# One fetch of six contiguous rows for both token tiles: re-pitching the relative-position bias table of a neighbourhood-attention layer

## The chip, the cores and the metric

The kernel runs on one core of one Trainium2 chip. The metric is the device time of one execution in microseconds (us). Beside it stands one execution under the hardware profiler. The engines are TensorE (PE, its weight load PEld), VectorE (DVE), ScalarE (ACT), GpSimd (POOL) and SyncE (SP). SP, POOL and ACT also start DMA transfers, which sixteen DMA engines carry out; q1 is the queue of the transfers that SP starts, q0 that of the transfers that POOL starts.

## The reference, cut to what matters

The model is two layers over 256 latent tokens (a grid of 4 rows by 64 columns) of width 1024, with 256 context tokens. The first layer mixes tokens by neighbourhood attention (8 heads of 64) and a short gated convolution; the second by a convolution of 31 taps; each is followed by a mixture of 16 experts. The bias table is used in the attention alone:

```
rpb_c = rpb.astype(jnp.float32)[:, :, dc]          # rpb: (8 heads, 15, 31)
...
    dr = rs + jnp.arange(kr) - r + (NA_KR_MAX - 1)
    bias = jnp.transpose(rpb_c[:, dr], (0, 2, 1, 3))
    s_loc = jnp.einsum("bwhd,brwkhd->bhwrk", q_r, k_nb).astype(jnp.float32) * scale + bias[None]
```

With 4 grid rows every query sees all 4, and the difference of grid rows lies between -3 and 3: seven of the fifteen table rows of a head are used. Inside a grid row a query sees 16 of the 64 columns; the kernel computes all 64 and adds a mask of -1e30 outside.

## The kernel before

Stage one of the kernel is the input projection. Its weights (w_in) and the modulation matrices (w_mod) come in units of 512 KB through one ring of eight slots, in an order written out by hand (FIRST): after the first six weight units, roughly three modulation units go to two weight units. SP issues the loads in that order; each waits until the unit eight places ahead of it has been consumed. ACT rounds a weight unit into whi (line 802), DVE computes the rest wlo (line 1101), and PE multiplies with both. There is room for six rounded units. The modulation vectors 2 to 4 are summed on DVE (lines 1116, 1119), 24 units in all; the others go through PE (line 1626). All three engines work through orders fixed in the program. The blocks of PE in order: two blocks for K (lines 1731 to 1733, the first in a form of its own, lines 1775 to 1777), two for V (lines 1750 to 1752, four tiles of 24 matmuls each), two for Q, two each for the three parts of the convolution (lines 1731 to 1733 again). ACT rounds up to the tenth weight unit (here n9, counted from n0) before it copies the four tiles of the first V block out of PSUM (line 893), rounds n10 and n11 after them, and rounds n12 and n13 only after the last tile of the second V block. PE may not start the second V block before those copies, since it has four PSUM banks for these tiles.

The bias goes this way. POOL loads the seven rows of each head into rpbt (56 partitions, line 722), waits until the second modulation unit is through, and writes rpbt into memory as bias_scratch, every partition 64 times (line 725). When that has landed it fetches bias (line 734): partition q of a half of the tile starts at another offset in bias_scratch, and so gets the table shifted by its column. One fetch covers one head, one token tile and one half, 64 partitions of four rows of 256 B. There are 32 fetches. DVE adds the mask to each head (mask_bias, line 1129), at places in its order given by MASK_AT: heads 0, 1, 2 ahead of n8's rest, 3 and 4 ahead of n9's, 5 ahead of n10's, 6 ahead of n12's, 7 ahead of n14's. The attention adds the bias to the scores (line 1251) and takes their maximum (line 1252). bias lies where the modulation vectors 2 to 5 are placed later; POOL fills vectors 2 to 4 (line 711) when all 16 scores have been multiplied. In the code n16 and so on follow the same count.

After the attention come the output projection, the router and the experts, whose weights stream through the same ring enlarged to 20 slots.

## Time and profile before

| | |
|---|---|
| median of 3 executions | 895.24 us (889.35 to 898.9) |
| the profiled execution | 895.48 us, its span 893.6 us |
| busy in the span: PE, DVE, ACT, POOL | 831.7, 402.4, 241.2, 83.1 us |
| mean granted TensorE clock | 0.96 |
| read from HBM | 291.77 MB |

Times in the rows below are counted from the start of the span. "Busy" counts what an engine executes; a wait shows as the idle time in brackets ahead of an instruction, with what ended it. Landing is the time from the issue of a DMA to the arrival of its data.

### The profile page before, as it was taken

How to read it: one execution, taken by the hardware profiler on the slowest of the kernel's cores; microseconds unless marked ns; L12 is line 12 of the kernel's file. 1: busy time of each engine (PE TensorE's matmuls, PEld its weight loads, DVE VectorE, ACT ScalarE, POOL GpSimd, SP SyncE). 2: the span in 40 equal slices, each digit the busy share in tenths (PEclk: the TensorE clock that was granted, in tenths of full speed). 3: DMA queues.
4: the chain of work that ended last, by engine and by line, in shares of the span. 5: the costliest groups of instructions: out<-in, count | busy, mean ns of one | idle time of the engine just before them, and what ended most of it. 6: DMA issues, size and time to landing. Idle time of an engine off the chain costs nothing.

```text
span 893.6 us, 16817 instructions
## 1 busy us (share of the span) xinstructions
PE 831.7 (93%) x6940; PEld 524.4 (59%) x6940; DVE 402.4 (45%) x682; ACT 241.2 (27%) x449; POOL 83.1 (9%) x154
## 2 busy tenths in 40 slices
PE   5898999999999899999997999989899899999994
PEld 3588995596655355554543987458555445554541
DVE  0476998746522223233336743456702222323334
ACT  3752535623111111111113533443121111111112
POOL 4180000013000000000000344200000000000000
PEclk9999999997799899999997999979899999999997
DMA  9999895869899999999998986599799999999993
GB/s 358 369 260 336 296 366 182 290 200 388 252 393 397 391 398 391 392 354 397 395 398 296 323 244 178 164 369 353 268 386 398 386 398 395 392 376 397 392 397 139
DMA packets 142158, 300.59 MB, mean 336 GB/s; under 512 B 12576, under 2 KB 43584, under 8 KB 142072
## 3 DMA queue, kind: packets, MB, share of 16 engines
q1 hardware_dynamic: 135360, 286.53, 88.5%
q0 software_dynamic: 6384, 12.76, 5.0%
q8 instruction: 59, 0.97, 0.5%
q14 instruction: 27, 0.22, 0.1%
q10 hardware_dynamic: 328, 0.11, 0.0%
HBM read 291.77 MB, written 2.92 MB: 330 GB/s over the span
## 4 chain that ended last, share of the span: by engine, by line
PE 74%; DMA 11%; DVE 8%; ACT 3%; issue 3%; SPq 0%; DVEq 0%; ACTq 0%
PE ps L2024 24%; PE ps L2049 12%; DMA ring<-in_moe_w 6%; PE ps L1975 5%; DMA ring<-in_w_mod 4%; PE ps L1945 3%; PE ps L2114 3%; PE ps L1946 3%; DMA ring<-in_na_w_in 2%; PE ps L1626 2%; PE ps L2140 2%; PE ps L2142 2%; PE ps L2141 2%; DVE wlo L1101 2%; PE ps L1750 1%
## 5 line engine op out<-in xcount | busy, mean ns | idle before, releaser
L2024 PE MATMUL ps<-ring,xg 128*64 128x256 f32 (+1 forms) x2432 | 252.0, 389 | 6.4 <-DMA ring<-in_moe_w 6.1
L2024 PEld LDWEIGHTS ps<-ring,xg 128*64 128x64 f32 (+1 forms) x2432 | 133.8, 129 | 95.3 <-issue 36.9
L1481 DVE SCALAR_TENSOR_TENSOR xres<-ps,gs,xres 128x512 f32<-128x512 f32 x128 | 90.0, 747 | 179.7 <-PE ps L1975 179.7
L2049 PE MATMUL ps<-ring,hidT 128*64 128x512 f32 (+1 forms) x608 | 119.2, 599 | 2.1 <-DMA ring<-in_moe_w 1.7
L2049 PEld LDWEIGHTS ps<-ring,hidT 128*64 128x64 f32 (+1 forms) x608 | 33.5, 128 | 68.9 <-issue 58.3
L1101 DVE TENSOR_TENSOR wlo<-ring,whi 128x1024 fp32r<-128x1024 f32 x56 | 66.6, 1220 | 15.3 <-ACT whi L802 15.2
L802 ACT CAST whi<-ring 128x1024 fp32r<-128x1024 f32 x56 | 56.7, 1046 | 52.4 <-DMA ring<-in_na_w_in 36.3
L969 ACT COPY xg<-ps 128x384 f32<-128x384 f32 (+2 forms) x44 | 20.6, 469 | 145.3 <-PE ps L1946 145.3
L1626 PE MATMUL ps<-ring,pair 128*32 128x256 f32 x576 | 47.2, 448 | 11.4 <-DMA ring<-in_w_mod 7.5
L1465 DVE TENSOR_TENSOR yg<-ps,g2keep 128x512 f32<-128x512 f32 x32 | 21.6, 689 | 74.0 <-PE ps L2049 74.0
L1945 PE MATMUL ps<-pick,hthi 128*128 128x192 f32 (+1 forms) x192 | 52.5, 310 | 0.0
L1945 PEld LDWEIGHTS ps<-pick,hthi 128*128 128x128 f32 x192 | 39.0, 203 | 16.4 <-issue 14.1
L1946 PE MATMUL ps<-pick,htlo 128*128 128x192 f32 (+1 forms) x192 | 48.0, 285 | 0.0
L982 ACT ACTIVATE silu<-ps 128x256 f32<-128x256 f32 x32 | 11.6, 382 | 124.7 <-PE ps L2024 124.7
L1459 DVE TENSOR_TENSOR hid<-silu,ps 128x256 f32<-128x256 f32 x32 | 12.9, 420 | 69.8 <-ACT silu L982 69.7
L1731 PE MATMUL ps<-hThi,whi 128*128 128x256 f32 (+1 forms) x144 | 42.4, 295 | 0.1
L1975 PE MATMUL ps<-yhi,spread 64*128 64x512 f32 (+1 forms) x152 | 37.4, 489 | 5.0 <-DVE ylo L1471 5.0
L1733 PE MATMUL ps<-hTlo,whi 128*128 128x256 f32 (+1 forms) x144 | 42.0, 291 | 0.0
L1732 PE MATMUL ps<-hThi,wlo 128*128 128x256 f32 (+1 forms) x144 | 41.9, 291 | 0.0
L988 ACT COPY hidT<-ps 128x256 f32<-128x256 f32 (+1 forms) x26 | 11.0, 422 | 114.6 <-PE ps L1996 114.6
L1946 PEld LDWEIGHTS ps<-pick,htlo 128*128 128x128 f32 x192 | 39.0, 203 | 1.0 <-issue 1.0
L2140 PE MATMUL ps<-fThi,whi 128*128 128x256 f32 x128 | 36.4, 285 | 0.7 <-DVE fTlo L1536 0.7
(265 smaller groups left out, 1311.9 us busy)
## 6 DMA issues: line engine op xcount, KB each, us to landing
ring<-in_moe_w SPq DMA_DIRECT2D x384, 512.0 KB, 11.6
ring<-in_w_mod SPq DMA_DIRECT2D x96, 512.0 KB, 7.4
ring<-in_na_w_in SPq DMA_DIRECT2D x24, 512.0 KB, 9.5
ring<-in_cf_pw_w SPq DMA_DIRECT2D x24, 512.0 KB, 8.2
ring<-in_ab_w_out SPq DMA_DIRECT2D x8, 512.0 KB, 5.1
mods<-mod_scratch POOLq DMA_DIRECT2D x8, 512.0 KB, 6.9
urep<-uT SPq DMA_DIRECT2D x64, 35.5 KB, 3.4
urep<-uT POOLq DMA_DIRECT2D x64, 35.5 KB, 3.2
```

Of the source, the lines that this page charges most:

```text
L802: A.copy(whi[:, n % SPL, :], raw_unit(u)).then_inc(w_rounded, 1)
L1101: V.tensor_tensor(wlo[:, n % SPL, :], raw_unit(u), whi[:, n % SPL, :], ALU.subtract).then_inc(unit_done, 1)
L1481: V.scalar_tensor_tensor(out=dst, in0=ps[:, plan.spread_banks(m, i)[half], :], scalar=gs[:, t, place:place + 1], in1=dst, op0=ALU.mult, op ...
L1626: ins = T.matmul(ps[q * QUAD:(q + 1) * QUAD, bank, 0:QW], pair[:, k, :], raw_unit(u)[:, q * QW:(q + 1) * QW], start=(k == 0), stop=(k == K ...
L1731: T.matmul(dst, wpart(n0, k, 0, m * P, P), acts(k, 0), start=(k == 0), stop=False)
L1733: i3 = T.matmul(dst, wpart(n0, k, 0, m * P, P), acts(k, 1), start=False, stop=(k == KC - 1))
L1945: T.matmul(dst, hthi[:, t, k * P:(k + 1) * P], sel, start=(t == 0), stop=False)
L1946: ins = T.matmul(dst, htlo[:, t, k * P:(k + 1) * P], sel, start=False, stop=(t == NT - 1))
L1975: ins = T.matmul(ps[:, plan.spread_banks(m, i)[half], :], spread[rows, m % 2, a, t * P:(t + 1) * P], part[rows, a, :], start=(a == 0 and p ...
L2024: ins = T.matmul(ps[lo:lo + width, BW[a], c0:c0 + 2 * P], tile[:, k, o:o + width], raw[:, p.slot(u), w0:w0 + 2 * P], start=(q == 0 and kk ...
L2049: ins = T.matmul(ps[lo:lo + width, BY[a], :], hidT[:, a, o:o + width], raw[:, p.slot(u), half * HALF:(half + 1) * HALF], start=(q == 0), s ...
L2140: T.matmul(dst, wpart2(done_n, k, 0, m * P, P), a0, start=(k == 0), stop=False)
```

## The change

The seven used rows of a head now lie one behind the other on one partition of rpbt (8 partitions of 512 elements), each 64 elements from the next (GRID_W, where the old layout gave a row 128 and a partition of its own). bias_scratch becomes 8 x 64 x 512. Since the rows of a head are at a pitch of 64, four grid rows by 64 columns are 256 contiguous elements, and the windows of the two token tiles overlap in one run of six rows, 384 elements: one fetch per head and half serves both tiles. There are 16 fetches of 64 partitions by one run of 1536 B. The tile has 384 elements a head instead of 512 (12 KB instead of 16 KB a partition), and the second tile reads at an offset 128 elements lower than the first. One DMA instead of eight loads the table. Since the last heads now lie under vector 4, its fill waits until the last bias has been added (biased) as well.

```
-        rpbt = at("rpbt", [HEADS * 7, P], 48)
+        rpbt = at("rpbt", [HEADS, BAND], 48)
...
-        bias = at("bias", [P, HEADS, NT, SEQ], 2 * D * 4 / 1024, base=mods_at)
+        bias = at("bias", [P, HEADS, NEAR * GRID_W], 2 * D * 4 / 1024, base=mods_at)
...
-            for h in range(HEADS):
-                eng.dma_start(rpbt[h * 7:(h + 1) * 7, 48:48 + 2 * KCOL - 1], na_rpb[0, h, 4:11, :]).then_inc(rpb_in, 16)
-            eng.wait_ge(rpb_in, 16 * HEADS)
+            bands = rpbt[:, GRID_W - KCOL:GRID_W - KCOL + OFFS * GRID_W].rearrange("h (r c) -> h r c", r=OFFS)[:, :, 0:2 * KCOL - 1]
+            eng.dma_start(bands, na_rpb[0, :, 4:4 + OFFS, :]).then_inc(rpb_in, 16)
+            eng.wait_ge(rpb_in, 16)
             eng.wait_ge(tensor_unit, 2 * KC)
-            eng.dma_start(bias_scratch, rpbt[:].unsqueeze(1).broadcast_to([HEADS * 7, GRID_W, P])).then_inc(rpb_out, 16)
+            eng.dma_start(bias_scratch, rpbt[:].unsqueeze(1).broadcast_to([HEADS, GRID_W, BAND])).then_inc(rpb_out, 16)
             def load_bias(h):
-                for t in range(NT):
-                    for half in range(2):
-                        src = bass.AP(tensor=bias_scratch.tensor, offset=(h * 7 + 3 - 2 * t - half) * GRID_W * P + GRID_W - 1,
-                                      ap=[[P - 1, GRID_W], [GRID_W * P, ROWS], [1, GRID_W]])
-                        dst = bias[half * GRID_W:(half + 1) * GRID_W, h, t, :].rearrange("p (r c) -> p r c", r=ROWS)
-                        eng.dma_start(dst, src).then_inc(bias_in[h], 16)
+                for half in range(2):
+                    src = bass.AP(tensor=bias_scratch.tensor, offset=h * GRID_W * BAND + (1 - half) * GRID_W + GRID_W - 1,
+                                  ap=[[BAND - 1, GRID_W], [1, NEAR * GRID_W]])
+                    eng.dma_start(bias[half * GRID_W:(half + 1) * GRID_W, h, :], src).then_inc(bias_in[h], 16)
...
             for v in range(2, 5):
+                if v == 4:
+                    eng.wait_ge(biased, 2 * HEADS)
                 mod_fill(v, mods[:, v * D:(v + 1) * D])
...
-                eng.wait_ge(bias_in[h], 64)
-                full = bias[:, h].rearrange("p t (r c) -> p (t r) c", r=ROWS)
-                mask = cst[:, C_MASK:C_MASK + GRID_W].unsqueeze(1).broadcast_to([P, NT * ROWS, GRID_W])
+                eng.wait_ge(bias_in[h], 32)
+                full = bias[:, h].rearrange("p (r c) -> p r c", r=NEAR)
+                mask = cst[:, C_MASK:C_MASK + GRID_W].unsqueeze(1).broadcast_to([P, NEAR, GRID_W])
                 V.tensor_tensor(full, full, mask, ALU.add).then_inc(bias_masked, 1)
...
-                link(V.tensor_tensor(local, local, bias[:, h, t, :], ALU.add))
+                link(V.tensor_tensor(local, local, bias[:, h, 2 * (1 - t) * GRID_W:2 * (1 - t) * GRID_W + SEQ], ALU.add))
```

The new constants are OFFS = 7, NEAR = 6 and BAND = 512; P is 128, ROWS is 4.

## Rows read from the trace of the kernel before

**Rows 1.** The chain that ended last, from 60 to 77 us: start, us, what.
```profile
54.60 20.74 DMA ring<-in_na_w_in
...
76.32 0.37 ACT vv L893
```

**Rows 2.** Timeline of ACT, 60 to 78 us; in brackets idle time and what ended it.
```profile
75.37 1.04 ACT L802 CAST whi<-ring 128x1024 fp32r<-128x1024 f32 x1 [8.60 <-DMA ring<-in_na_w_in]
```

**Rows 3.** Timeline of PE (matmuls), 71 to 90 us.
```profile
72.34 0.28 PE L1751 MATMUL ps<-wlo,hThi 128*128 128x256 f32 x1
72.45 0.28 PE L1752 MATMUL ps<-whi,hTlo 128*128 128x256 f32 x1
76.83 0.36 PE L1750 MATMUL ps<-whi,hThi 128*128 128x256 f32 x1 [4.10 <-ACT vv L893]
```

**Rows 4.** Windows: stretch, length, busy (count) of PE, PEld, DVE, ACT, POOL, clock, DMA share, GB/s.
```profile
48.00:72.50 24.50, 24.41 (x155) 21.66 (x153) 16.62 (x16) 8.04 (x11) 19.83 (x32) 1.00 1.03 260
76.80:119.20 42.40, 42.37 (x354) 41.31 (x355) 36.01 (x41) 17.73 (x30) 0.63 (x1) 0.96 0.95 332
119.20:140.00 20.80, 20.79 (x174) 18.64 (x173) 19.99 (x37) 7.13 (x11) 0.60 (x1) 1.00 0.78 277
```

**Rows 5.** The same view, in stretches of 2 us after PE's stop.
```profile
76.00:78.00 2.00, 1.17 (x9) 1.20 (x10) 1.56 (x2) 1.50 (x5) 0.00 (x0) 0.92 1.06 394
78.00:80.00 2.00, 2.00 (x11) 2.00 (x11) 2.00 (x3) 1.05 (x1) 0.00 (x0) 0.50 1.04 379
80.00:82.00 2.00, 2.00 (x15) 2.00 (x14) 2.00 (x3) 0.00 (x0) 0.00 (x0) 0.73 1.06 378
```

**Rows 6.** DMA view, 49.1 to 75.4 us: totals, queues, bias fetches.
```profile
DMA packets 3693, 6.83 MB, mean 260 GB/s; under 512 B 673, under 2 KB 2488, under 8 KB 3691
...
q1 hardware_dynamic: 2625, 4.63, 68.9%
q0 software_dynamic: 1066, 2.17, 34.4%
...
bias<-bias_scratch POOLq DMA_DIRECT2D x32, 64.0 KB, 7.0
```

**Rows 7.** DMA view, 75.4 to 89 us: totals.
```profile
DMA packets 2949, 5.21 MB, mean 383 GB/s; under 512 B 159, under 2 KB 2186, under 8 KB 2948
```

**Rows 8.** Timeline of POOL around the write and the fetches.
```profile
32.14 1.70 POOL L725 DMA_DIRECT2D bias_scratch<-rpbt  x1 [22.07 <-PE ps L1626]
49.06 19.83 POOL L734 DMA_DIRECT2D bias<-bias_scratch  x32 [13.20 <-DMA bias_scratch<-rpbt]
175.87 1.81 POOL L711 DMA_DIRECT2D mods<-mod_scratch  x3 [30.31 <-PE ps L1616]
```

**Rows 9.** DMA view, 37 to 43 us: POOL's queue (packets, MB, share of 16 engines).
```profile
q0 software_dynamic: 373, 1.25, 58.0%
```

**Rows 10.** Timeline of DVE around 88 us, the instructions before and after its idle time.
```profile
85.64 0.68 DVE L1129 TENSOR_TENSOR bias<-bias,cst 128x512 f32<-128x512 f32 x1
90.97 1.23 DVE L1101 TENSOR_TENSOR wlo<-ring,whi 128x1024 fp32r<-128x1024 f32 x1 [4.65 <-ACT whi L802]
```

**Rows 11.** The instructions that touch bias: durations min/median/max ns, first and last start.
```profile
L1251 DVE TENSOR_TENSOR ps<-ps,bias x16: 421/426/433, 126.6 to 177.8; 128x256 f32<-128x256 f32 x16
L1129 DVE TENSOR_TENSOR bias<-bias,cst x8: 683/685/691, 62.1 to 100.4; 128x512 f32<-128x512 f32 x8
```

**Rows 12.** Timeline of DVE, 178 to 204 us.
```profile
178.28 0.69 DVE L1252 TENSOR_REDUCE smx<-ps 128x1 f32<-128x512 f32 x1
203.34 1.23 DVE L1171 TENSOR_TENSOR htok<-xres,mods 128x1024 f32<-128x1024 f32 x1
```

**Rows 13.** The page's DMA issues: the fills of the modulation vectors.
```profile
mods<-mod_scratch POOLq DMA_DIRECT2D x8, 512.0 KB, 6.9
```

**Rows 14.** Windows, columns as in rows 4: the router's end, and the experts.
```profile
230.00:240.00 10.00, 10.00 (x74) 7.23 (x75) 5.55 (x18) 1.87 (x3) 0.00 (x0) 0.77 0.56 205
300.00:380.00 80.00, 77.25 (x588) 39.81 (x588) 23.66 (x36) 10.44 (x23) 0.00 (x0) 0.96 1.04 394
```

More of the change, by code:

```diff
@@ L22 @@
 ROWS = SEQ // GRID_W
+OFFS = 2 * ROWS - 1
+NEAR = OFFS - 1
+BAND = 8 * GRID_W
 HEADS = 8
@@ L2266 @@
     args.append(nc.dram_tensor("in_consts", [P, C_N], F32, kind="ExternalInput").ap())
-    args.append(nc.dram_tensor("bias_scratch", [HEADS * 7, GRID_W, P], F32, kind="Internal").ap())
+    args.append(nc.dram_tensor("bias_scratch", [HEADS, GRID_W, BAND], F32, kind="Internal").ap())
     args.append(nc.dram_tensor("mod_scratch", [MODS, D], F32, kind="Internal").ap())
```

## The prediction

> **What bounds the kernel now.** I read the chain that ended last first, in the stretch where the bias is made and fetched. From 54.60 to 75.34 us it stands on one DMA, a unit of w_in that took 20.74 us to land; then come ACT's rounding of it and ACT's copy of V out of PSUM [rows 1]. ACT's timeline says the same: it sat idle 8.60 us for that unit (n9) [rows 2]. ACT copies the first V tiles only after n9, and PE needs those copies, so PE stops at the end of the first V block: its last matmul starts at 72.45, the next at 76.83 [rows 3]. The matmuls there start 0.11 us apart [rows 3], so PE could have gone on at 72.57: 4.26 us are lost. Then the clock: in the 6 us after the stop the granted clock was 0.92, 0.50 and 0.73 [rows 5], after full clock up to the stop [rows 4]. At full clock the missing shares, 0.08, 0.50 and 0.27 of 2 us each, are 1.7 us. So the stop costs PE 4.26 + 1.7 = 6.0 us.
>
> Second, the windows on both sides. From 48 to 72.5 PE is busy 24.41 of 24.50 us, and from 76.8 to 119.2 it is busy 42.37 of 42.40 [rows 4]. So nothing else is to be had from PE there, and nothing stands between the stop and 119 us that could swallow what the stop gives back. From 119.2 to 140 DVE is the full one, 19.99 of 20.80 us. DVE's own timeline shows where it last had room: it idles 4.65 us until 90.97, and what ends that is ACT's rounding of n12 [rows 10], which in ACT's order comes behind the last copy of the second V block, that is, behind PE. DVE's order from there on is work without a gap, hung on a point set by PE. If PE is 6 us earlier, so is that point.
>
> Third, why n9 is late. From 49.1 to 75.4 us the DMA engines are full, yet move 260 GB/s [rows 6]; as soon as the bias fetches are in, they move 383 GB/s [rows 7]. In that stretch lie the 32 fetches, 64 KB each in rows of 256 B.
>
> **The fetches, removed and added.** Before: 32 x 65.5 KB = 2.10 MB, in 8192 rows. The stretch of 26.3 us moved 6.83 MB, so 4.73 MB of other data, which at 383 GB/s need 12.3 us. The fetches therefore cost 14.0 us of all DMA engines (at 383 GB/s they would cost 5.5). After: 16 x 98.3 KB = 1.57 MB in 1024 rows of 1536 B. Lower bound, at 383 GB/s: 4.1 us; the rate of rows 7 was reached mostly by rows of w_in, 1 KB each, so rows of 1.5 KB are near that end, and I take 4.5. Upper bound, if the price goes by bytes as it does now: 14.0 x 1.57/2.10 = 10.5 us. So 9.5 us of DMA time come free, at least 3.5, and all ahead of n9's landing. n9 was issued at 54.60, which stays; it lands at about 66 instead of 75.34, at the worst at 71.8. The limit for PE is 72.57 less ACT's chain from landing to PE, 76.83 - 75.34 = 1.49 us, so 71.1. The likeliest value clears it by 5 us, and the upper bound misses it by 0.7 us. The stop goes, and with it most likely the dip in the clock, since the rows show it only behind the stop. On PE: -6.0 us; at the upper bound -3.5 to -5.3.
>
> POOL issues 16 fetches instead of 32, at 0.62 us each [rows 8] about 9.9 instead of 19.83 us, so the last fetch goes out about 10 us earlier; nobody stands behind it in POOL's queue until the first modulation row, tens of us later. Nothing on the path.
>
> **The write to bias_scratch.** Before: issued at 32.14, landed when the first fetch goes at 49.06 [rows 8]. It shrinks from 56 x 64 rows of 512 B (1.84 MB) to 8 x 64 rows of 2 KB (1.05 MB), but it reads 8 partitions instead of 56. In the middle of the write q0 moved 1.25 MB in 6 us, 208 GB/s, with 58% of the engines, so 22 GB/s for each busy engine [rows 9]. No row shows such a write from 8 partitions. The lower bound is by bytes, 16.9 x 0.57 = 9.6 us. If at most eight engines can take part, each has 131 KB, just what 14 engines had each in the write before, and the write takes about as long as now. I take 14 to 17 us, so the fetches begin between 46 and 49: cost nought, at most 1 us of gain, since the bias is not what n9 waits for. The upper bound is by partitions: 208 x 8/56 = 30 GB/s, 35 us. That is a rival below. The Trainium skill speaks against this part of the change ("SBUF — State Buffer", section on the DMA port swizzle): DMA bandwidth goes by the SBUF ports that the partitions reach, 27 GB/s each; 56 partitions reach eight ports, partitions 0 to 7 two. By that estimate the write would need 19 us at 54 GB/s and land near 56. The 208 GB/s of rows 9 lie just under its figure for eight ports, 218, so this trace cannot refute it.
>
> **Loading the table.** One DMA instead of eight on POOL, which waits for PE until 32.14 afterwards anyway, 22.07 us idle [rows 8]. Nothing.
>
> **The masks.** 128x512 took 0.685 us, 128x256 took 0.426 [rows 11]; a straight line gives 0.556 for 384 elements, 0.13 us less for each of eight. Six or seven fall where DVE waits anyway (ahead of 90.97), one, head 7's, in the full stretch: -0.13 us. The addition at line 1251 keeps its shape.
>
> **The new wait.** POOL now holds the fill of vector 4 until the last maximum, which ends at 178.97 [rows 12] where it went out at about 177.1 (third of three from 175.87, rows 8): 2 us later. Behind it on POOL's queue are the move of vector 5, whose row DVE makes only during the output projection, and what follows it. Vector 4 is first read at 203.34 [rows 12]; with a landing of 6.9 us [rows 13] it is there at about 187. Cover 16 us, cost nought; without that cover it would be the 2 us.
>
> **Does the gain reach the end?** From 230 to 240 the DMA engines are only 0.56 busy while the router finishes: the expert units that may be fetched early are in, and the ring stands full. From there the experts run at 394 GB/s with a full DMA [rows 14], a fixed amount of work hung on the router's end. An earlier router moves all of it. So the sum: -6.0 - 0.1 = -6.1 us against the profiled execution's own 895.48, which lies 0.2 above the median. Forecast 895.24 - 6.2 = 889.0 us.
>
> **Rivals.**
> (A) The fetches cost by bytes, so the change does only part of what it says: -3.5 to -5.3, 890 to 892 us. For it: the DMA engines' records give q0 34.4% for its 2.17 MB, no worse per byte than q1 [rows 6]. Against: then the rate would not have leapt from 260 to 383.
> (B) The gain is taken over by DVE and the ring. From 76.8 to 119.2 DVE is busy 36.0 of 42.4 and the DMA share is 0.95 [rows 4]; with 6 us less on the clock, the slots may not be full when n12 is due, and DVE waits for loads instead. The check: DVE reached the point ahead of n12 at 86.32 [rows 10] and n12 would be due at 84.9; it must gain 1.4 us, and it is given 9.5 us of DMA. If only half the gain survives, 892; if none, 895.
> (C) Slower: the write is paced by the partitions it reads. At 30 GB/s it lands near 71 instead of 49. The first three heads come 11 us later, 82 (six fetches issued at 0.62 us, and 7.0 us to land, rows 6 and 8). DVE stands at their masks, in its order ahead of n8's rest; from those masks to n9's rest it has 7.6 us of work (five masks at 0.56, two rests and two modulation units at about 1.2 each), so PE's Q block starts at 89.5, no earlier than now, and DVE, with another 8.2 us until n12 (two rests, four modulation units, two masks), comes there at 98 instead of 90.97: +7, 902 us. It decides from a landing at about 65 on (33 us after issue, against 16.9 now): up to there DVE's idle time pays. The port rule of the Trainium skill lands the write at 56, short of that point, where the bias's lateness costs DVE nothing; the ring's loads on the engines that read those partitions would be held up, and n9 would land at about 71 to 72. By it the time would be 889 to 892; its chance is one in six.
> (D) The stop's removal brings more, because earlier landings also shorten later waits: against it stand the full rows of PE on both sides. 884 to 887.
>
> **Chances.** Forecast as it stands (887 to 891) 0.52; A and the mild form of the write together 0.20; B 0.12; C 0.05; D 0.11. Single executions differ by 1% (889.35 to 898.9), so about 1% is what a measurement can tell from no change, and medians may be off by 2 to 3 us. The range of 8 in 10 is 884 to 895.5: it leaves out C, the worst of B and the far end of D. Faster by over 1% (under 886.3) 0.22, within 1% 0.72, slower by over 1% 0.06.
>
> **What would show it.** In the profile after: 16 fetches; the stretch from 50 to 70 us at 350 GB/s or more; no wait of 8.60 us of ACT at n9; PE busy 2.00 of 2.00 through 72 to 77 with the clock at 1.00 up to 84; the first rounding after the second V block at 83.8 instead of 89.89; the last addition of bias at 171.7 instead of 177.8. A landing of the write after 56, or a wait of DVE at the masks, would show C or its mild form; an idle DVE between 85 and 119 would show B. The prediction is wrong altogether if the stop is gone and the end has not moved.

## The result, and the profile after

The changed kernel took 898.53 us (median of 20 executions, 889.83 to 902.9), the kernel before 893.19 (20 executions on the same chip, 885.17 to 900.0). The ratio is 1.0057, with a 95% interval of 1.0033 to 1.0082: slower by 0.6%, where 0.7% faster was forecast. The profiled execution took 900.92 us, its span 899.2, that is 5.6 us more than before.

POOL's timeline of the changed kernel answers to [rows 8]; in brackets idle time and what ended it.

```profile
32.55 0.82 POOL L728 DMA_DIRECT2D bias_scratch<-rpbt  x1 [25.56 <-PE ps L1629]
58.10 8.68 POOL L735 DMA_DIRECT2D bias<-bias_scratch  x16 [22.66 <-DMA bias_scratch<-rpbt]
184.63 0.53 POOL L714 DMA_DIRECT2D mods<-mod_scratch  x1 [2.27 <-DVE smx L1255]
```

The write is issued at 32.55 and has landed by 58.10, after 25.3 us in the DMA view, where it took 16.6 before, although it carries 1.05 MB instead of 1.84. The fetches are half as many and are out in 8.68 us instead of 19.83, as forecast. The third line is the new wait ahead of vector 4's fill, 2.27 us long.

What the DMA engines did meanwhile stands in the DMA view from 38 to 50 us (queues: packets, MB, share of the time of 16 engines).

```profile
DMA packets 936, 1.89 MB, mean 158 GB/s; under 512 B 208, under 2 KB 588, under 8 KB 935
q0 software_dynamic: 361, 0.83, 51.7%
q1 hardware_dynamic: 574, 1.05, 26.1%
```

The same stretch of the kernel before, for comparison, since no row ahead of the prediction shows it:

```profile
DMA packets 1486, 3.80 MB, mean 317 GB/s; under 512 B 168, under 2 KB 737, under 8 KB 1485
q0 software_dynamic: 641, 2.24, 59.7%
q1 hardware_dynamic: 844, 1.55, 37.1%
```

q0 holds about the same share of the engines (52% against 60%) and moves 0.83 MB with it instead of 2.24. And q1, the ring's queue, falls from 1.55 to 1.05 MB. The write is not only slow, it makes the ring slow. The windows of the changed kernel answer to [rows 4, 5] (stretch, length, busy (count) of PE, PEld, DVE, ACT, POOL, clock, DMA share, GB/s):

```profile
44.00:46.00 2.00, 2.00 (x7) 1.51 (x6) 1.39 (x5) 2.00 (x5) 0.00 (x0) 0.50 0.75 104
50.00:60.00 10.00, 10.00 (x44) 8.09 (x44) 2.02 (x2) 0.84 (x2) 1.90 (x4) 1.00 0.71 160
74.00:76.00 2.00, 0.00 (x0) 0.00 (x0) 0.37 (x1) 1.44 (x3) 0.00 (x0) 0.50 1.06 361
76.00:78.00 2.00, 1.86 (x8) 1.86 (x9) 2.00 (x3) 1.43 (x3) 0.00 (x0) 0.50 1.10 362
78.00:80.00 2.00, 2.00 (x12) 2.00 (x11) 2.00 (x5) 0.19 (x1) 0.00 (x0) 0.50 0.92 343
80.00:82.00 2.00, 2.00 (x16) 2.00 (x16) 1.79 (x2) 0.97 (x2) 0.00 (x0) 0.79 0.93 336
82.00:119.20 37.20, 37.20 (x328) 36.12 (x327) 33.25 (x40) 15.55 (x28) 0.62 (x1) 1.00 0.90 309
```

From 76.14 on PE is full again, as it was from 76.83 on before; full clock comes back at 82. SP's timeline says how the slow write reaches the ring. After:

```profile
35.79 14.33 SPq L607 DMA_DIRECT2D ring<-in_w_mod  x2
50.16 5.43 SPq L611 DMA_DIRECT2D ring<-in_na_w_in  x1
55.63 2.99 SPq L607 DMA_DIRECT2D ring<-in_w_mod  x1
58.66 0.43 SPq L611 DMA_DIRECT2D ring<-in_na_w_in  x1
```

Before:

```profile
49.40 0.38 SPq L608 DMA_DIRECT2D ring<-in_na_w_in  x1
50.53 0.33 SPq L604 DMA_DIRECT2D ring<-in_w_mod  x1
51.67 0.38 SPq L608 DMA_DIRECT2D ring<-in_na_w_in  x1
```

These are the units n7 and n8. SP's issue of n7, 0.38 us long before, takes 5.43 us, and n8 goes out at 58.66 instead of 51.67. The chain that ended last, which answers to [rows 1], now runs through n7:

```profile
48.52 1.64 DVE wlo L1104 x2
50.16 24.37 DMA ring<-in_na_w_in
74.58 0.92 issue
75.51 0.59 ACT kT L890
76.14 0.58 PE ps L1753
```

n7 needs 24.37 us to land; before it needed 8.8. ACT's timeline (answers to [rows 2]), the casts of n6 and n7 and what stands behind them:

```profile
62.35 1.05 ACT L805 CAST whi<-ring 128x1024 fp32r<-128x1024 f32 x1 [0.78 <-DMA ring<-in_na_w_in]
74.56 1.04 ACT L805 CAST whi<-ring 128x1024 fp32r<-128x1024 f32 x1 [11.16 <-DMA ring<-in_na_w_in]
75.51 1.07 ACT L890 COPY kT<-ps 128x512 f32<-128x512 f32 x2
```

ACT rounds n6 and n7 between the second and the third copy of K out of PSUM, so the last two copies wait for n7. PE's timeline (answers to [rows 3]):

```profile
68.93 0.28 PE L1755 MATMUL ps<-whi,hTlo 128*128 128x256 f32 x1
76.14 0.58 PE L1753 MATMUL ps<-whi,hThi 128*128 128x256 f32 x1 [6.94 <-ACT kT L890]
```

So the stop is not gone. It stands after two of the four tiles of the first V block instead of at the block's end, and it has grown: PE could have gone on at 69.04 (0.11 us behind its last matmul) and goes on at 76.14, 7.10 us against 4.26. It goes on a little earlier than before, but with two more tiles ahead of it. The clock is at 0.50 from 74 to 80 and at 0.79 to 82. DVE's timeline (answers to [rows 10]):

```profile
77.97 1.49 DVE L1132 TENSOR_TENSOR bias<-bias,cst 128x384 f32<-128x384 f32 x3
92.57 0.55 DVE L1132 TENSOR_TENSOR bias<-bias,cst 128x384 f32<-128x384 f32 x1
96.33 1.23 DVE L1104 TENSOR_TENSOR wlo<-ring,whi 128x1024 fp32r<-128x1024 f32 x1 [3.21 <-ACT whi L805]
```

The rest of n12 starts at 96.33 instead of 90.97: 5.36 us later. And the instructions that touch bias (answers to [rows 11]; min/median/max ns, first and last start):

```profile
L1132 DVE TENSOR_TENSOR bias<-bias,cst x8: 550/551/554, 78.0 to 105.8; 128x384 f32<-128x384 f32 x8
L1254 DVE TENSOR_TENSOR ps<-ps,bias x16: 421/425/433, 132.0 to 183.2; 128x256 f32<-128x256 f32 x16
```

The first addition of bias starts at 132.0 instead of 126.6, the last at 183.2 instead of 177.8. Both are 5.4 us later, and the span is 5.6 us longer: in this pair of executions the whole loss is made before 97 us.

Not all of it is the stop. PE resumes its first K block at 42.34 instead of 41.95 (0.39 us). The longer stop adds 2.84 us and the longer stretch at a low clock behind it some 0.65 (2.35 us of missing clock against 1.7). The rest, 1.7 us, is a dip of the clock from 42 to 48 us (0.82, 0.50 and 0.82; the first window above shows its middle), which this execution has and the one of the kernel before has not. The four make 5.6 us, against the 5.4 of n12. The dip comes and goes with the execution, as e8 and e12 show below, so these two profiles put some 3.5 us of the loss on the longer stop. The medians of 20 executions are 5.3 us apart, and how often each kernel has the dip isn't known.

### The profile page after: what moved, and what is told of

It is laid out like the page before. It is cut to its first block, busy times and chain, and to the rows that moved or that the text cites. A ratio compares the mean times of both kernels' runs of the same rounds, so it can differ in the third digit from the quotient of the medians.

```text
span 899.2 us, 16795 instructions
## 1 busy us (share of the span) xinstructions
PE 830.7 (92%) x6940; PEld 523.6 (58%) x6940; DVE 401.1 (45%) x682; ACT 241.7 (27%) x449; POOL 67.9 (8%) x131
## 4 chain that ended last, share of the span: by engine, by line
PE 70%; DMA 14%; DVE 9%; issue 3%; ACT 3%; SPq 0%; DVEq 0%; ACTq 0%
PE ps L2027 23%; PE ps L2052 12%; DMA ring<-in_moe_w 6%; PE ps L1978 5%; DMA ring<-in_w_mod 4%; PE ps L2117 3%; PE ps L1948 3%; DMA ring<-in_na_w_in 3%; PE ps L1949 2%; PE ps L1629 2%; PE ps L2143 2%; PE ps L2145 2%; PE ps L2144 2%; PE ps L1753 1%; PE ps L1754 1%
## 5 line engine op out<-in xcount | busy, mean ns | idle before, releaser
L2052 PE MATMUL ps<-ring,hidT 128*64 128x512 f32 (+1 forms) x608 | 121.1, 605 | 1.7 <-DMA ring<-in_moe_w 1.2
L1629 PE MATMUL ps<-ring,pair 128*32 128x256 f32 x576 | 44.6, 429 | 12.9 <-DMA ring<-in_w_mod 8.8
L1948 PE MATMUL ps<-pick,hthi 128*128 128x192 f32 (+1 forms) x192 | 49.0, 295 | 0.0
L1948 PEld LDWEIGHTS ps<-pick,hthi 128*128 128x128 f32 x192 | 36.8, 191 | 16.4 <-issue 14.1
L1949 PE MATMUL ps<-pick,htlo 128*128 128x192 f32 (+1 forms) x192 | 45.0, 274 | 0.0
L1949 PEld LDWEIGHTS ps<-pick,htlo 128*128 128x128 f32 x192 | 36.7, 191 | 0.5 <-issue 0.5
```

The lines of the kernel that those rows point to most:

```text
L1629: ins = T.matmul(ps[q * QUAD:(q + 1) * QUAD, bank, 0:QW], pair[:, k, :], raw_unit(u)[:, q * QW:(q + 1) * QW], start=(k == 0), stop=(k == K ...
L1948: T.matmul(dst, hthi[:, t, k * P:(k + 1) * P], sel, start=(t == 0), stop=False)
L1949: ins = T.matmul(dst, htlo[:, t, k * P:(k + 1) * P], sel, start=False, stop=(t == NT - 1))
L2052: ins = T.matmul(ps[lo:lo + width, BY[a], :], hidT[:, a, o:o + width], raw[:, p.slot(u), half * HALF:(half + 1) * HALF], start=(q == 0), s ...
```

## The experiments

Two questions were open: why the write takes 25.3 us, and what the fetches would bring without it. For the write, theory G says that it is paced by groups of four neighbouring partitions that it reads: partitions 0 to 7 are two groups. Theory N says that the number of partitions counts, or that each of eight engines has its share. Theory F puts the loss on the fetches, whose longer rows would hold the engines longer. The table gives what each run showed. "Landing" is the time from the issue of the write to its landing in the DMA view, "38 to 50" and "50 to 60" are the rates of all transfers in those stretches (in most runs the second is that of the fetches), "n12" the start of its rest on DVE, "first add" that of line 1251's (1254's) first instruction. The ratio is to the kernel before on the same chip.

| kernel | landing us | 38 to 50, GB/s | 50 to 60, GB/s | n12 | first add | ratio [95%] |
|---|---|---|---|---|---|---|
| before | 16.6 | 317 | 268 | 90.97 | 126.6 | 1 |
| after | 25.3 | 158 | 160 | 96.33 | 132.0 | 1.0057 [1.0033, 1.0082] |
| e1, every 4th partition | 12.6 | 318 | 238 | 87.39 | 123.2 | 0.9917 [0.9882, 0.9952] |
| e2, every 2nd | 14.9 | 264 | 260 | 87.09 | 122.9 | 0.9909 [0.9876, 0.9943] |
| e9, every 16th | 15.2 | 279 | 251 | 85.23 | 120.9 | 0.9941 [0.9920, 0.9962] |
| e3, before with 8 partitions | 40.9 | 121 | 61 | | 153.8 | 1.0315 [1.0265, 1.0364] |
| e4, 16 copies | 10.5 | 363 | 266 | 88.58 | 124.2 | 0.9931 [0.9900, 0.9962] |
| e7, e4 with rows 2048 B apart | 9.6 | 355 | 282 | | 122.1 | one execution |
| e5, 16 copies, 128-partition fetch | 13.9 | 384 | 378 | 86.48 | 122.1 | 0.9945 [0.9918, 0.9972] |
| e8, copies, old fetch | 11.4 | 380 | 249 | 87.79 | 123.4 | 0.9999 [0.9966, 1.0033] |
| e12, e8 again | 11.5 | 382 | 257 | 87.40 | 123.0 | 0.9950 [0.9910, 0.9990] |
| e10, 4 copies, 128-partition fetch | 13.7 | 384 | 377 | 86.34 | 122.2 | 0.9908 [0.9869, 0.9947] |
| e11, after with ACT's copies first | 25.6 | 144 | 158 | | 129.3 | 0.9985 [0.9948, 1.0023] |
| e13, before again | 16.7 | 318 | 266 | 91.88 | 127.5 | one execution |

**e1: the same eight partitions' worth of data on partitions 0, 4, ..., 28.** Bytes, rows, fetches and the number of source partitions are those of the changed kernel.

```
-        rpbt = at("rpbt", [HEADS, BAND], 48)
+        rpbt = at("rpbt", [HEADS * 4, BAND], 48)
...
-            bands = rpbt[:, GRID_W - KCOL:...
+            bands = rpbt[0:HEADS * 4:4, GRID_W - KCOL:...
...
-            eng.dma_start(bias_scratch, rpbt[:].unsqueeze(1)...
+            eng.dma_start(bias_scratch, rpbt[0:HEADS * 4:4].unsqueeze(1)...
```

> The changed kernel, with the eight heads' rows of the table on partitions 0, 4, 8 ... 28 instead of 0 to 7; the same 8 partitions of source, the same 1.05 MB, nothing else. Theory G (the write is paced by the groups of neighbouring partitions that it reads; partitions 0 to 7 are two groups of four, here it is eight): the changed kernel's write took 25.3 us from issue to landing, here it takes 10 to 15 us, lands at 43 to 48, and the ring keeps over 300 GB/s between 38 and 50 us instead of 61 to 257. ACT no longer waits 9 us for a weight unit at 50 us. PE's stop shrinks; the time is that of the kernel before or up to 6 us under it, 887 to 893, ratio to before 0.994 to 1.000. Theory N (eight source partitions mean that eight DMA engines carry the whole write, wherever they lie): the landing stays within 2 us of 25.3 and the ratio stays at 1.006. Theory F (the longer runs of the fetch are what hurts): likewise no change.

POOL's timeline of e1, then its window and an issue of SP's:

```profile
32.51 0.82 POOL L728 DMA_DIRECT2D bias_scratch<-rpbt  x1 [25.52 <-PE ps L1629]
45.42 8.47 POOL L735 DMA_DIRECT2D bias<-bias_scratch  x16 [10.03 <-DMA bias_scratch<-rpbt]
```

```profile
38.00:50.00 12.00, 10.11 (x38) 7.68 (x37) 9.32 (x23) 11.97 (x22) 4.58 (x9) 0.86 0.92 318
```

```profile
49.73 0.38 SPq L611 DMA_DIRECT2D ring<-in_na_w_in  x1
```

and the ring's queue from 38 to 50 us in the DMA view:

```profile
q1 hardware_dynamic: 1044, 2.07, 51.5%
```

The spacing alone takes the landing from 25.3 to 12.6 us, the rate from 158 to 318 GB/s and SP's issue of n7 back to 0.38 us; the ring's queue moves 2.07 MB instead of 1.05. PE has no wait of half a microsecond or more from 45 to 125 us. The kernel is 0.8% faster than before, with the fetches as the change makes them, and faster than expected (0.994 to 1.000). This execution has the dip of the clock from 42 to 48 us too, as the changed kernel's had, so the two compare directly: n12 comes 8.94 us earlier by the spacing alone. F falls: the same fetches stand here. N falls too, since there are eight source partitions in both.

**e2: partitions 0, 2, ..., 14.** The edit is e1's with 2 in place of 4; it reads four groups.

> As the kernel with heads at every fourth partition, but on partitions 0, 2, 4 ... 14: four groups of four instead of two (changed kernel) or eight. Theory G: by the two-group write (25.3 us, of which some 5 are fixed and 20 go by the rate) half of 20 and 5 fixed, a landing 14 to 17 us after issue, between the other two or equal to the eight-group one if the engines, not the groups, are the limit by then. Theory N: 25 us.

```profile
47.41 8.80 POOL L735 DMA_DIRECT2D bias<-bias_scratch  x16 [12.29 <-DMA bias_scratch<-rpbt]
```

The write, issued at 32.23, landed after 14.9 us, between the two. The time does not tell it from e1.

**e3: the kernel before, its table on eight partitions.** Fetches, bytes (1.84 MB) and everything else stay those of before; only a head's seven rows lie on one partition, at the old pitch of 128.

```
-        rpbt = at("rpbt", [HEADS * 7, P], 48)
+        rpbt = at("rpbt", [HEADS, 7 * P], 48)
...
-            eng.dma_start(bias_scratch, rpbt[:].unsqueeze(1).broadcast_to([HEADS * 7, GRID_W, P])).then_inc(rpb_out, 16)
+            eng.dma_start(bias_scratch, rpbt[:].unsqueeze(1).broadcast_to([HEADS, GRID_W, 7 * P])).then_inc(rpb_out, 16)
...
+                                      ap=[[7 * P - 1, GRID_W], [P, ROWS], [1, GRID_W]])
```

> The kernel before with one thing of the change alone: the table lies on partitions 0 to 7 (seven rows of 128 elements each) and the write reads these 8 partitions; the bytes written stay at 1.84 MB and the 32 fetches of four rows of 256 B stay as they were. Theory G: 1.84/1.05 x 20 + 5 = 40 us from issue to landing instead of 16.6, the ring crawls for as long, DVE stands at the first masks, time 10 to 20 us above before, ratio 1.01 to 1.025. Theory F: as before, within 0.3%, since the fetch is unchanged. Theory N gives the same as G here if eight engines are slow in themselves.

POOL's timeline of e3 up to 90 us (27 of the 32 fetches), and its window in the middle of the write:

```profile
73.62 17.02 POOL L734 DMA_DIRECT2D bias<-bias_scratch  x27 [38.24 <-DMA bias_scratch<-rpbt]
```

```profile
50.00:60.00 10.00, 10.00 (x46) 8.20 (x45) 2.03 (x2) 1.05 (x1) 0.00 (x0) 1.00 0.49 61
```

The write takes 40.9 us, the kernel 3.15% more, beyond the 1 to 2.5% that were expected. This is the loss by itself, without any other part of the change: PE stops for 14.9, 4.1 and 6.4 us. It also gives the price. After and e3 both read two groups; 0.52 and 0.92 MB a group took 25.3 and 40.9 us, so 0.393 MB more took 15.6 us: 25 GB/s a group, and some 4.5 us besides. For four groups that gives 0.262 / 0.0252 + 4.5 = 14.9 us, as measured in e2, and for eight groups 9.7. e1 measured 12.6; the DMA share is 0.92 there, so the write probably waits for the ring's transfers as well, which no run separates.

The Trainium skill ("SBUF — State Buffer", the section on the DMA port swizzle) gives 27 GB/s for each port and puts partitions 0 to 7 on two of them; the 25 GB/s of these runs agree. It also says that partitions 32 apart share a port.

**e9: partitions 0, 16, ..., 112.** By G in its plain form these are eight groups, as in e1. By the port map just named they are four ports, as in e2.

```
-            bands = rpbt[:, ...
+            bands = rpbt[0:HEADS * 16:16, ...
```

> The changed kernel with the heads at every sixteenth partition, 0, 16 ... 112. If any spacing of four or more gives each head a way of its own, the write lands 12.6 us after issue as with every fourth partition, and from 38 to 50 us 318 GB/s are moved. If the SBUF's groups are those of the Trainium skill (page SBUF - State Buffer, the DMA port swizzle: partitions 32 apart share a port, so these eight reach four ports), it lands as with every second partition: 14.9 us, 264 GB/s. On the time no difference that can be measured, ratio 0.988 to 0.996.

```profile
38.00:50.00 12.00, 10.08 (x44) 7.88 (x43) 9.32 (x22) 11.97 (x21) 2.25 (x5) 1.00 0.89 279
```

15.2 us and 279 GB/s are e2's figures (14.9, 264), not e1's (12.6, 318). So it is the port map's grouping that counts, not nearness as such. These are differences of 2.6 us and 39 GB/s between single executions. DVE's timeline of e9 at the place of [rows 10]:

```profile
85.23 1.23 DVE L1104 TENSOR_TENSOR wlo<-ring,whi 128x1024 fp32r<-128x1024 f32 x1 [3.06 <-ACT whi L805]
```

90.97 to 85.23 is -5.74 us. The first and the last addition of bias come 5.7 us earlier (120.9, 172.1), and the span, 888.0, is 5.6 us shorter.

**e4: sixteen copies of the table on 128 partitions,** each written four times: the same bytes, from every group.

```
+COPIES = 16
...
+            for i in range(COPIES):
+                bands = rpbt[i:P:COPIES, ...
...
+            eng.dma_start(bias_scratch.rearrange("h (i j) b -> (h i) j b", i=COPIES), rpbt[:].unsqueeze(1).broadcast_to([P, GRID_W // COPIES, BAND])).then_inc(rpb_out, 16)
```

> The changed kernel, but the table is loaded 16 times, so that a head's rows stand on 16 neighbouring partitions (128 in all), each written 4 times; the same 1.05 MB in memory, the same fetches. Theory G and N both: all engines and all groups take part, the write lands 7 to 12 us after issue. The difference to the kernel with every fourth partition tells what the engine count adds: under G alone nothing or 1 to 3 us of landing. Time: if the fetches of 1.5 KB cost 5 us less of all DMA engines than before (8.8 against 14.0 of the trace), PE's stop of 4.3 us and the dip of its clock mostly go: 887 to 890, ratio 0.993 to 0.997. If the fetches are no cheaper, ratio 0.999 to 1.001.

The fastest write but one, 10.5 us, and no better time than e1. The sixteen small loads of the table cost time at the start: the second modulation unit is through later, the write went out at 34.40 instead of 32.55, n7 at 51.72 instead of 49.40, and that moves everything behind it. In the five runs with sixteen loads (e4, e5, e7, e8, e12) PE resumes its first K block 1.5 to 2.3 us later than before, in e10 with four loads 0.5; by which way the loads do it, no run shows. The rate while the fetches run stays low:

```profile
50.00:60.00 10.00, 10.00 (x46) 8.19 (x45) 9.00 (x8) 5.51 (x8) 3.58 (x7) 1.00 1.05 266
```

266 GB/s, and 238 in e1, are what the kernel before had (268) with rows of 256 B; the prediction had hoped for 350 or more from rows of 1536 B. Two theories: L, the rows start 2044 B apart in memory and are not aligned; H, each fetch fills 64 partitions, that is half of the groups.

**e7: e4 with the fetched rows 2048 B apart.** This leaves out the shift of the bias from partition to partition, so that every partition gets the same window.

```
-                                  ap=[[BAND - 1, GRID_W], [1, NEAR * GRID_W]])
+                                  ap=[[BAND, GRID_W], [1, NEAR * GRID_W]])
```

> The run with 16 copies, with the fetched rows 2048 B apart instead of 2044, so that all rows of a fetch start at the same place within 256 B. It leaves out the shift of the bias from partition to partition, so its scores are not those of the reference. Theory L: the fetch stretch goes from 266 to 350 GB/s or more. Theory H: it stays at 240 to 280.

```profile
50.00:60.00 10.00, 9.92 (x44) 7.84 (x43) 8.52 (x8) 4.72 (x7) 1.75 (x4) 1.00 1.05 282
```

282 GB/s: alignment brings 16 of the 117 GB/s that are missing to the 383 of [rows 7]. L falls as the main cause. The one execution took 890.07 us.

**e5: e4 with every row written 128 times** (2.10 MB), so that one fetch can fill 128 partitions. There are eight fetches of 192 KB, with the same bytes and rows.

```
+                src = bass.AP(tensor=bias_scratch.tensor, offset=h * P * BAND + P - 1,
+                              ap=[[BAND - 1, P], [1, NEAR * GRID_W]])
+                eng.dma_start(bias[:, h, :], src).then_inc(bias_in[h], 16)
```

> The run with 16 copies, but with 128 instead of 64 repetitions of a head's row in memory (2.1 MB written from 128 partitions), so that one fetch of 128 partitions by 1536 B replaces the two of 64: 8 fetches in all. Theory H (a fetch into 64 partitions reaches half of the groups of partitions and so holds all DMA engines to about 250 GB/s): the stretch of the fetches shows 350 GB/s or more. Theory L (the rows start off a boundary, since they lie 2044 B apart): it stays at 240 to 280 GB/s. On the time nothing, since PE has no stop left between 48 and 125 us in the run with 16 copies: ratio 0.991 to 0.996.

```profile
50.00:60.00 10.00, 9.90 (x44) 7.81 (x43) 8.57 (x9) 5.47 (x8) 1.96 (x4) 1.00 1.05 378
```

378 GB/s, as H expects. The fetches are also half as many and twice as large as in e4, and the memory rows are repeated 128 times; no run keeps their number and widens them alone, so that it is the partitions reached is the likeliest reading and not shown by itself. At that rate the 1.57 MB cost 4.2 us, the 4.5 that the prediction took. The time is 0.55% below before's and no better than e1's: the stop was gone already, and a DMA queue that is faster still releases nobody. n12 stands at 86.48, 4.49 us earlier; PE resumed its first K block, after a wait of 1.9 us inside it that all kernels have, 1.46 us later than before (43.41 against 41.95), again with the sixteen loads, so the stop itself gave back 5.95.

**e8: the write spread, the fetches of before.** Table on 128 partitions in 16 copies, 1.84 MB, 32 fetches of 64 KB.

```
-            eng.dma_start(bias_scratch, rpbt[:].unsqueeze(1).broadcast_to([HEADS * 7, GRID_W, P])).then_inc(rpb_out, 16)
+            eng.dma_start(bias_scratch.rearrange("h (i j) b -> (h i) j b", i=16), rpbt[:].unsqueeze(1).broadcast_to([P, GRID_W // 16, 7 * P])).then_inc(rpb_out, 16)
```

> The kernel before with its 32 fetches of four rows of 256 B, its 16 KB tile and its 1.84 MB of bytes written, but the table stands on 128 partitions (16 copies of each head) for the write, as in the run with 16 copies. It separates the two halves of the change: against that run (ratio 0.993) it differs in the fetch, against the kernel before in the write alone. If the shorter fetches of the change are worth what the trace suggests (DMA cost 14 us before, some 9 after), PE still stops at the V blocks here: write landed 3 us earlier than before at most, ratio to before 0.996 to 1.000, ACT waits 5 us or more at n9. If the gain of the run with 16 copies came from the write alone, the ratio here is 0.993 too and PE doesn't stop.

The write landed after 11.4 us instead of 16.6, and the profile shows no stop of PE: n9 is rounded from 73.6 on instead of 75.37, and PE itself is later, since it resumed the first K block 1.57 us later and then had the dip of the clock (1.7 us from 44 to 48). But the ratio is 0.9999, with executions from 882.61 to 899.52: the ratio is that of the first case of the expectation, the trace that of the second. The profiled one was the fastest of them, so its trace says little of the median.

**e12: e8 once more,** to see where its spread is made: in this stage, by a stop that comes and goes (S), or elsewhere (T).

> The run with the old fetch and the write from 128 partitions once more, since its profiled execution (882.6 us, no stop of PE, n9 rounded at 67.58) was its fastest of 12, and its median was that of before. Theory S: with the old fetch n9 lands within a few us of the limit of 71, so that some executions have the stop and others not; a slower execution under the profiler should then show n9 rounded after 71 and PE idle. Theory T: the spread is made elsewhere; then the profile shows no stop again even at 890 us or more, and the longer time is in the experts' stretches.

The rounding at 67.58 is that of n8; n9's is the one at 73.6.

PE's timeline of e12 shows the one wait from 45 to 125 us:

```profile
74.87 0.36 PE L1751 MATMUL ps<-whi,hThi 128*128 128x256 f32 x1 [0.65 <-ACT vv L894]
```

The windows from 44 to 46 us of e8 and of e12, which are the same kernel:

```profile
44.00:46.00 2.00, 2.00 (x7) 1.57 (x6) 1.78 (x6) 2.00 (x5) 0.64 (x2) 0.54 1.05 278
44.00:46.00 2.00, 2.00 (x10) 1.66 (x9) 1.77 (x7) 2.00 (x6) 0.67 (x2) 1.00 1.05 284
```

One execution has the dip of the clock in the first K block, the other has not.

A median of 890.85 and 0.995. The two profiled executions differ by 8.7 us in span (880.8, 889.5) and by 0.4 us at the first addition of bias; from 640 to 880 us PE is busy 223.9 us in one and 232.5 in the other. So the difference of these two is made in the experts (T). What the write alone is worth in the median stays open between nothing and 0.9%. In this stage it takes nearly all of the stop away by itself, with the old fetches in place: n9, issued 1.58 us later than before, is in 1.97 us earlier, e12 keeps 0.76 of the 4.26 us of idle PE, and no low clock follows.

**e10: both halves put right at a lower price:** four copies of each head on every fourth partition, 128 repetitions, eight fetches of 128 partitions, four table loads.

```
+                bands = rpbt[4 * i:P:4 * COPIES, ...
...
+            eng.dma_start(bias_scratch.rearrange("h (i j) b -> (h i) j b", i=COPIES), rpbt[0:P:4].unsqueeze(1).broadcast_to([HEADS * COPIES, P // COPIES, BAND])).then_inc(rpb_out, 16)
```

> The version that the runs point to. Each head's rows stand on four partitions, every fourth of the 128, so the write reads all sixteen groups with 32 partitions and the table needs four small loads instead of sixteen; 128 repetitions in memory (2.1 MB) and 8 fetches of 128 partitions by 1536 B, as in the run with the full fetch. The write lands 9 to 14 us after issue, the fetch stretch runs at 350 GB/s or more, PE has no stop from 48 to 120 us. Ratio to before 0.989 to 0.995, against the kernel with every fourth partition no difference that can be told; if the sixteen small loads cost the full-fetch run 1 to 2 us at its start, this one gets them back.

0.9908, 886.17 us: the lowest ratio of all, and not to be told from e1's 0.9917, which needs three changed lines. Landing (13.7 us), fetch stretch (377 GB/s) and PE without a stop are as expected.

**e11: the changed kernel with ACT's order turned,** a test of how the slow write reaches PE. All K copies go ahead of the rounding of n6 and n7, and two V copies ahead of n8 and n9.

```
-                if n % 2 == 1:
-                    round_upto(6 + n + 1)
+                if n == 3:
+                    round_upto(8)
...
+                if n == 1:
+                    round_upto(10)
```

> The changed kernel, its slow write and all, with the order of ACT altered: the last K copies out of PSUM come ahead of the rounding of n6 and n7, and the first two V copies ahead of n8 and n9. In the changed kernel PE stood 6.94 us for such a copy, which was queued behind the wait for n7 (landed at 74.5). If that order is what turns a late unit into lost time, PE now runs through the first V block to about 72 and stops only until n7's rest at about 77: 2 to 4 us come back, ratio to before 1.001 to 1.004. If the lateness of the units costs by itself, whatever the order, the ratio stays at 1.006.

The timeline of PE in e11, its longest wait:

```profile
77.89 0.38 PE L1755 MATMUL ps<-whi,hThi 128*128 128x256 f32 x1 [3.28 <-DVE wlo L1106]
```

The write is as slow as ever (25.6 us, 144 GB/s), but the stop falls from 6.94 to 3.28 us, now for n7 itself, with three short ones behind it (0.90, 1.30 and 0.37 us), and the clock stays at 1.00 from 76 to 84 us. The first addition comes at 129.3 instead of 132.0, and the ratio is 0.9985, better than the 1.001 to 1.004 expected. Against the changed kernel's 1.0057, which was measured beside other executions of before, that is 0.7% less. Of the 1.4% that lie between the changed kernel and e1 that is about half (by ratios whose intervals are 0.25 to 0.37% wide to each side), and at the first addition it is 2.7 of 8.8 us. So a part of the loss comes by the copies' place in ACT's order, and the rest by the late landing itself.

**e13: the kernel before, a second look.**

> The kernel before, unchanged, for a second look: whether its stop of PE at 72.5 us (4.26 us, with the dip of the clock behind it) is there in another execution. Theory S allows 2 to 8 us of stop and a time that follows it; theory T expects 4 us again whatever the time.

The stop is there again: PE is idle for 3.90 us until 76.88, and the clock is 0.50 from 76 to 82. 896.48 us, n12 at 91.88 (90.97), the first addition at 127.5 (126.6), the last at 182.7 (177.8). Up to the first addition two executions agree within 1 us; from there to the last they can part by 4 us.

## Why the prediction was wrong

**The step that failed: the write to bias_scratch, "cost nought".** The prediction took 14 to 17 us for it, on the thought that eight engines would each have as many bytes as fourteen had before. It took 25.3, and e1 to e3 show that the source's groups set it. About eight engines were indeed held (52% of 16 from 38 to 50 us), but each moved 8 GB/s, not the 22 of [rows 9]. The upper bound, 35 us by partitions, held it. The port rule that the prediction cited came near with a landing at 56, against 58. Its 19 us from 32.14 on make only 51; 56 is right with the 4.5 us beside the rate that e3 showed later, and the prediction does not name them. What was wrong there was the effect. The prediction asked only when the bias would come, found it in time for DVE up to a landing at 65, and let the ring's loads lose so little that n9 would come at 71 to 72 and the time at 889 to 892. In the trace the bias is in time (no wait of DVE at the masks), and what the write costs, it costs through the ring: q0 held 52% of the engines for 69 GB/s, q1 got 88 GB/s (129 before), and SP's own issues blocked for 5 to 14 us. It was n7 that came late, two w_in units before n9, and it stopped PE for 7.10 us. The kernel with the same source spread (e1) has no stop. The dip of the clock that adds 1.7 us in the profile of the changed kernel was in no term of the sum, and is not tied to the slow write, since e1 has it too.

**The stop of PE costs 6.0 us.** Right. Where it is gone (e9) n12 comes 5.74 us earlier, 5.94 once its K block's later resumption (42.15 against 41.95) is taken out, and 5.95 in e5 in the same way. Neither has the dip from 42 to 48, as before hasn't. The prediction's 171.7 us for the last addition was 172.1 in e9, and e9's ratio of 0.9941 (0.9920 to 0.9962) holds the forecast's 0.993. So the price of the stop stood, but the change as it was did not remove it; with the table spread it went. Its going was closer than forecast: n9 was in at 70.85 in e9, against the prediction's 66 and its limit of 71.1. And the fetches alone were not the reason for its lateness: with the write spread and the old fetches (e12) all but 0.76 us of the stop went as well.

**The fetches, 4.5 us.** Too low; Rival A had the better of it. In the stretch from 60 to 74 us of the changed kernel (DMA view; answers to [rows 6]):

```profile
DMA packets 2007, 3.86 MB, mean 276 GB/s; under 512 B 318, under 2 KB 1403, under 8 KB 2006
q1 hardware_dynamic: 1244, 2.28, 59.6%
q0 software_dynamic: 762, 1.57, 44.7%
```

2.28 MB at the 383 GB/s of [rows 7] need 6.0 of the 14.0 us, so the fetches cost 8.0; by bytes it would have been 10.5. That leaves 6 us of DMA time free instead of 9.5. The error was to put the price on the length of the rows: in e5 the same rows, fetched into 128 partitions at a time, cost 4.2.

**Does the gain reach the end?** In two pairs of executions it does: +5.4 us at both ends of the additions and +5.6 in the span of the changed kernel, -5.7 and -5.6 in e9. Single spans are a weak test of it, since the experts alone part e8 and e12 by 8 us, and e1's span is 10.3 us shorter for 3.4 us at the first addition. The ratios are the better evidence: e8 apart, every version whose stop is gone or under 1 us is 0.5 to 0.9% below before. Rival B (DVE and the ring absorb it) did not show.

**The small terms.** A mask of 384 elements took 0.551 us (0.556 forecast). The new wait held vector 4's fill for 2.27 us (2 forecast), and nothing waited for it. One load of the table instead of eight gave and cost nothing that shows, and sixteen cost 1.5 to 2.3 us (e5, e4).

**The chances.** 0.06 for slower by over 1% counted only a bias too late for DVE, and the mild form was priced as a smaller gain. That the ring's loads could lose more than the fetches gave back had no price and no chance. The measured loss of 0.6% lies within 1%, but outside the range, whose upper end of 895.5 stopped short of it.

## What to carry to other kernels

A DMA between memory and a few neighbouring partitions is priced twice: its own time, and the time for which it holds DMA engines that other queues need. Before packing a source onto fewer partitions, ask which transfers run beside it and what waits for those; if the data must be small, put its rows four partitions apart (12.6 us here, against 25.3 side by side; sixteen apart gave 15.2). A stop of an in-order engine can be read off the trace and believed, but what removes it must be followed through every queue that shares the DMA engines, from the first unit on, not only to the unit that was late before.

## What the runs showed of the hardware

- A write of 1.05 MB from 8 partitions took 25.3, 14.9 or 12.6 us, by their spacing alone (1, 2, 4); with a spacing of 16 it took 15.2. From two groups of partitions it ran at 25 GB/s a group.
- While it ran from two groups, the transfers of another queue ran at 88 GB/s (1.05 MB from 38 to 50 us), where before had 129 (1.55 MB) and e1, whose write had landed by 45.1, had 172 (2.07 MB). The DMA share was 0.78, and in e3, from 50 to 60 us, 0.49 with 61 GB/s in all. The Trainium skill tells of stalled writes that stall an engine's other queues, for transfers between cores ("DMA: Bandwidth & Descriptors", the section on back-pressure in remote DMA); here it shows inside one core and with the reading side as the narrow one. Which of the two sides holds the engine was not tried.
- Issuing slows down too while such a write runs: two loads on SP took 14.33 us to issue instead of 6.19, and one 5.43 instead of 0.38.
- Fetches into 64 partitions kept the whole traffic at 238 to 282 GB/s whether their rows had 256 or 1536 B; into 128 partitions, half as many and twice as large, it was 377 and 378.
- The granted clock fell to between 0.50 and 0.60 for some of the time from 42 to 50 us, inside PE's first K block, in after, e1, e2, e3, e4, e8 and e11, and stayed at 1.00 there in before, e5, e7, e9, e10, e12 and e13. PE had been idle for 1.9 us before it in all of them. e8 and e12 are the same kernel, so one kernel can run with the dip and without it; what brings it stays open. By the missing shares in after and in e1 (0.82, 0.50 and 0.82 of three stretches of 2 us) it is worth 1.7 us.
